# Sums of squares at five joints: six tiles added on GpSimd, three products of ones in place of eight

## The reference

```python
def rmsnorm_2(x, g):
    xf = x.astype(jnp.float32)
    y = xf * lax.rsqrt(jnp.mean(xf * xf, -1, keepdims=True) + EPS)
    return (y * g.astype(jnp.float32)).astype(x.dtype)

def macaron_half_ffn(x, pre_g, post_g, w_gate, w_up, w_down):
    h = rmsnorm_2(x, pre_g)
    h = (jax.nn.silu(h @ w_gate) * (h @ w_up)) @ w_down
    return x + 0.5 * rmsnorm_2(h, post_g)
...
    for i in range(DEPTH_2):
        p = layers[i]
        x = macaron_half_ffn(x, *p["ffn1"])
        pre_g, post_g = p["norms"]
        x = x + rmsnorm_2(p["mixer"](rmsnorm_2(x, pre_g), *p["mix"]), post_g)
        x = macaron_half_ffn(x, *p["ffn2"])
```

## Time and profile before

| | us |
|---|---|
| median of 3 runs | 2516.71 |
| lowest and highest run | 2516.51, 2528.49 |
| profiled execution, first to last instruction (span) | 2449.2 |
| median less span | 67.5 |
| TensorE busy in the span | 2190.0 (89%) |
| VectorE busy | 1628.7 (66%) |
| ScalarE busy | 997.5 (41%) |
| GpSimd busy | 541.4 (22%) |

### The profile page before, as it was taken

The page is one execution under the profiler, slowest core; times in us unless marked ns, Lnnn a source line. Parts: engine busy times, 40 slices in busy tenths (PEclk is TensorE's granted clock), DMA queues, the critical chain, the costliest instruction groups (busy, mean ns, idle before and its releaser), DMA issues. The chain is left out here.

```text
span 2449.2 us, 40856 instructions
## 1 busy us (share of the span) xinstructions
PE 2190.0 (89%) x16086; PEld 1805.2 (74%) x16086; DVE 1628.7 (66%) x3155; ACT 997.5 (41%) x1896; POOL 541.4 (22%) x549
## 2 busy tenths in 40 slices
PE   8988998877877777777999999999999898999998
PEld 7987998733332333224999988999999777888998
DVE  6675755766666676644766766666766777648666
ACT  5553535523333333333444445434444563024343
POOL 0000001877777777772100000000000000000000
PEclk9999999998899999999999999999999999999999
DMA  5530453899999999994655432655455432003653
GB/s 202 181 118 2 146 186 107 268 410 409 409 409 409 409 409 404 410 409 165 188 183 185 154 104 69 191 183 185 142 185 184 129 105 77 3 3 102 190 183 111
DMA packets 140319, 509.45 MB, mean 208 GB/s; under 512 B 15969, under 2 KB 16609, under 8 KB 139745
## 3 DMA queue, kind: packets, MB, share of 16 engines
q1 hardware_dynamic: 65824, 237.32, 30.4%
q0 software_dynamic: 73728, 268.47, 27.6%
q10 hardware_dynamic: 576, 1.05, 0.2%
HBM read 505.72 MB, written 1.05 MB: 207 GB/s over the span
## 5 line engine op out<-in xcount | busy, mean ns | idle before, releaser
L197 ACT ACTIVATE weights_high<-weights 128x1024 fp32r<-128x1024 f32 x436 | 460.2, 1059 | 532.5 <-PE ps L233 401.0
L231 PE MATMUL ps<-moving_high,weights_high 128*128 128x256 f32 x2224 | 639.8, 288 | 6.1 <-DVE moving_low L1277 3.0
L2284 PE MATMUL ps<-v_rows,subkeys 128*128 128x512 f32 x1024 | 494.7, 636 | 167.9 <-ACT subkeys L2338 167.9
L233 PE MATMUL ps<-moving_high,weights_low 128*128 128x256 f32 x2224 | 630.3, 283 | 0.0
L232 PE MATMUL ps<-moving_low,weights_high 128*128 128x256 f32 x2224 | 630.2, 283 | 0.0
L205 DVE TENSOR_TENSOR weights_low<-weights,weights_high 128x1024 fp32r<-128x1024 f32 x419 | 513.2, 1227 | 171.2 <-ACT weights_high L197 168.5
L2284 PEld LDWEIGHTS ps<-v_rows,subkeys 128*128 128x128 f32 x1024 | 200.6, 203 | 460.8 <-issue 460.7
L2444 DVE CUSTOM_DVE_ANT_0 u_rows<-u_rows,ps 128x1024 f32<-128x1024 f32 x256 | 308.9, 1219 | 233.2 <-DMA u_rows<-in_peer_u,experts 232.8
L231 PEld LDWEIGHTS ps<-moving_high,weights_high 128*128 128x128 f32 x2224 | 427.4, 192 | 11.4 <-issue 8.5
L232 PEld LDWEIGHTS ps<-moving_low,weights_high 128*128 128x128 f32 x2224 | 427.5, 192 | 0.6
L233 PEld LDWEIGHTS ps<-moving_high,weights_low 128*128 128x128 f32 x2224 | 427.1, 192 | 0.0
(11 more groups left out here) (569 smaller groups left out, 3198.2 us busy)
## 6 DMA issues: line engine op xcount, KB each, us to landing
weights<-in_l_ffn SPq DMA_DIRECT2D x264, 512.0 KB, 4.0
weights<-in_w_in SPq DMA_DIRECT2D x44, 512.0 KB, 4.0
weights<-in_l_in SPq DMA_DIRECT2D x24, 512.0 KB, 3.7
weights<-in_l_rkv SPq DMA_DIRECT2D x24, 512.0 KB, 3.6
weights<-in_w_ckv SPq DMA_DIRECT2D x16, 512.0 KB, 4.4
weights<-in_w_pq SPq DMA_DIRECT2D x16, 512.0 KB, 4.1
weights<-in_w_up_pair SPq DMA_DIRECT2D x8, 512.0 KB, 3.5
weights<-in_w_mix_out SPq DMA_DIRECT2D x8, 512.0 KB, 4.4
```

The source lines that it names most:

```text
L197: act.activation(self.high[:, c % SPLIT, :], self.raw[:, c % RING, :], ACT.Copy)\
L231: pe.matmul(out, lhs.high, rhs.high, start=start, stop=False)
L233: return pe.matmul(out, lhs.low, rhs.high, start=False, stop=stop)
L2284: last = pe.matmul(k.ps[:, 2 * tb + half, :], diagonal[:, i % DIAGONALS, :], v_rows[:, i % V_RING, 512 * half:512 * half + 512], start=i < ...
```

## The change

In each joint GpSimd now adds the squares of the first six tiles into tile 0, by five additions of 128x256: 1 to 0, then 3 to 2 and 2 to 0, then 5 to 4 and 4 to 0, each pair as soon as ScalarE has made its squares. TensorE makes no sums ahead of t = 2 and t = 4; ahead of t = 6 it waits for the last squares, makes the products of ones for tiles 6 and 7, waits for `six_added`, and makes the one for the sum of the six. `nsa_mixer`'s stage gets a GpSimd part that it did not have (`has_pool`).

```diff
--- before.py
+++ after.py
@@ -522,7 +522,7 @@
 
 
     order = (0, 1, 2, 4, 5, 6, 7, 3)
-    roots_first = False
+    roots_first, has_pool = False, True
     chunks = NSA_CHUNKS
     gain = "l0_mix_pre_g_2"
     GATES, CONV, CONV_GATE, KEYS, VALUES, QUERIES = (4, 5), 4, 12, 16, 18, 20
@@ -550,6 +550,9 @@
         h, tb = self.items[i]
         g = h // NSA_REP
         return h, tb, g, h % NSA_REP, P * (tb + 1), slice(64 * g, 64 * g + 64), slice(P * tb, P * tb + P)
+
+    def pool(self, pool, S):
+        late_parts_pool(pool, Front(S), self.squares)
 
     def ready(self, n):
         return n + 1
@@ -952,7 +955,7 @@
 
 
     order = range(KT)
-    roots_first = True
+    roots_first, has_pool = True, False
     chunks = 0
 
     def __init__(self, k, ctx, m, parts):
@@ -1084,6 +1087,11 @@
                 act.wait_ge(S["sum_ready"], 1)
                 act.activation(root[:, :], k.ps[:, sum_bank, 0:T], ACT.Sqrt, bias=k.eps(), scale=1.0 / D)\
                    .then_inc(S["root_ready"], 1)
+
+            if make.has_pool:
+                @block.gpsimd
+                def _(pool):
+                    make.pool(pool, S)
 
             @block.tensor
             def _(pe):
@@ -2452,17 +2460,14 @@
     keep_warm(k, pe, 6, 3)
     first_three = [k.w.arrived(pe) for _ in range(3)]
 
-    def sums(q):
-        pe.wait_ge(S["squares_ready"], q + 1)
-        for t in (2 * q, 2 * q + 1):
-            last = pe.matmul(k.ps[:, sum_bank, 0:T], k.const("ones"), squares[:, t, :], start=t == 0, stop=t == KT - 1)
-        return last
-
     for t in range(KT):
-        if t in (2, 4, 6):
-            sums(t // 2 - 1)
         if t == 6:
-            sums(3).then_inc(S["sum_ready"], 1)
+            pe.wait_ge(S["squares_ready"], 4)
+            for i in (6, 7):
+                pe.matmul(k.ps[:, sum_bank, 0:T], k.const("ones"), squares[:, i, :], start=i == 6, stop=False)
+            pe.wait_ge(S["six_added"], 1)
+            pe.matmul(k.ps[:, sum_bank, 0:T], k.const("ones"), squares[:, 0, :], start=False, stop=True)\
+              .then_inc(S["sum_ready"], 1)
         pe.wait_ge(S["parts_ready"], t + 1)
         for bank, tiles in enumerate(first_three):
             last = product(pe, k.ps[:, bank, 0:T], tiles[:, t, :], parts[:, t, :], start=t == 0, stop=t == KT - 1)
@@ -2476,6 +2481,20 @@
         for t in (2 * q, 2 * q + 1):
             act.activation(parts.high[:, t, :], src[:, t, :], ACT.Copy, scale=k.column(gain, t)).then_inc(S["high_ready"], 1)
         act.activation(squares[:, 2 * q:2 * q + 2, :], src[:, 2 * q:2 * q + 2, :], ACT.Square).then_inc(S["squares_ready"], 1)
+
+
+def late_parts_pool(pool, S, squares):
+    own = Steps(pool, S["pool_steps"])
+    for q in range(3):
+        pool.wait_ge(S["squares_ready"], q + 1)
+        own.did(pool.tensor_tensor(squares[:, 2 * q, :], squares[:, 2 * q, :], squares[:, 2 * q + 1, :], ALU.add))
+        own.settle()
+        if q:
+            added = pool.tensor_tensor(squares[:, 0, :], squares[:, 0, :], squares[:, 2 * q, :], ALU.add)
+            if q == 1:
+                own.did(added)
+            else:
+                added.then_inc(S["six_added"], 1)
 
 
 def late_parts_vector(k, v, S, src, gain, parts, update):
@@ -2668,6 +2687,7 @@
 
             @block.gpsimd
             def _(pool):
+                late_parts_pool(pool, S, squares)
                 if final:
                     pool.wait_ge(S["own_scale"], 1)
                     for q in range(4):
```

## The result

| | before | changed |
|---|---|---|
| median of 17 runs each, us | 2523.31 | 2530.98 |
| lowest to highest, us | 2515.06 to 2530.53 | 2516.24 to 2538.95 |
| profiled execution: time, us | not given | 2530.26 |
| profiled execution: span, us | 2449.2 | 2528.5 |

The ratio is 1.0037, with a 95% interval of 1.0026 to 1.0047: the change costs 9.3 us (6.6 to 11.9); the two medians differ by 7.7. Forecast were -0.15 us, 2516.6, and a range from 2510 to 2523. The loss was missed.

The account below looks back on a forecast made before the run. TensorE was taken as the late engine in the joints, VectorE having some three us to spare. Three FFN joints at 0.0, nsa_mixer +2.0 and l0_ffn1 -2.15 gave -0.15 us, on the median 2516.6 us, range 2510 to 2523.

Parts of the forecast that it names:

- What is removed: TensorE, all five joints: ten records of ones fewer per joint, 2.15 us each joint, 10.75 us in all, the ceiling.
- what is added: GpSimd, all five joints: five additions of 128x256 per joint, 25 in all, which stop VectorE.
- the stop of 0.54 us: VectorE in the joints: each GpSimd addition of 256 elements stops it 0.54 us, with ends 0.49 and 1.08.
- rival 3: Joints: the whole addition locks VectorE, 0.76 us each; FFN joints lose 0.2, nsa_mixer 3.1; +1.6, 2518.3 us; chance 0.12.
- The walk through an FFN joint: Joints before l0_ffn2, l1_ffn1, l1_ffn2: VectorE 2.0 us later, TensorE reaches tile 6 at 1362.24 against 1362.23; gain 0.0 each.
- rival 2: Joints: additions stop VectorE longer, 1.08 us each; FFN joints 1.5 us later, nsa_mixer loses 4.7; +7.0, 2523.7 us; chance 0.08.
- l0_ffn1: Joint where TensorE is far behind and VectorE has slack: the chain behind it moves ahead as a whole, -2.15 us.
- nsa_mixer's +2.0: Behind tile 6 of nsa_mixer's joint TensorE waits for VectorE, so all of VectorE's 2.0 us delay arrive: +2.0 us.
- rival 4: nsa_mixer and three FFN joints: new idle time lowers TensorE's clock, 1.56 us per fall; +6.2, 2522.8 us; chance 0.07.
- TensorE's freed time could not have been used here: nsa_mixer's joint: TensorE waits for VectorE behind tile 6, so freed time brings nothing even without GpSimd.
- Those 67.5 us lie outside of the span: Whole program: median 2516.71 us lies 67.5 above the profiled span of 2449.2, outside it and untouched by the change.
- No case reaches 12.6 us: Whole program: no rival nor the 10.75 us ceiling reaches 0.5%, 12.6 us; faster 0.02, slower 0.03, same 0.95.

Follow-up runs that it names:

- the run without additions: Changed kernel with all GpSimd additions dropped, so squares of tiles 1 to 5 are left out of the norm; ratio 1.0006 is not its own: 0.9979.
- the filled stop: Changed kernel with five unused identity products on TensorE where it stands still in nsa_mixer, ahead of the fifth weight chunk; ratio 1.0006 (0.9992 to 1.0020).

## Why the prediction was wrong

- **What is removed, what is added, and the stop of 0.54 us**: right. 0.55 each was measured, four of them, the fifth in ScalarE's shadow. Three rows from the begin of the trace, far from the joints, and the order of work written out, were enough. The rule quoted from the Trainium skill, page SBUF — State Buffer, section "SBUF: two separate sides", agrees with the trace in that one of the two blocks the other. But the fastest record of an addition is 0.740 us, and what it takes from VectorE is 0.55, so not the whole instruction, as far as GpSimd's records go, which are rough. That was rival 3, and it did not happen.
- **The walk through an FFN joint**: right, within 0.1 us in all three, and the run without additions shows that it is these stops that eat the 2.1 us.
- **The sums of rivals 2 and 3**: wrong. In the walk VectorE 2.0 us late leaves an FFN joint where it was, so each us beyond is lost. Rival 3 has VectorE 3.1 us late, which is 1.1 us a joint and not 0.2, and some +4.2 in all; rival 2 has 4.7, which is 2.7 a joint and not 1.5, and some +10.6. Neither happened, but both were priced too low.
- **l0_ffn1**: right, 2.16 us sooner for 2.15. The stage's own length moved by 2.8, of which nothing can be made, since it varies by 1.7 with nothing changed.
- **nsa_mixer's +2.0**: right as a wait (0.41 to 2.51 us) but it was put down as the stage's whole loss, and **this is the step that failed**: "All of VectorE's 2.0 us arrive at TensorE: +2.0 us", with nothing for the clock in the sum. The stage lost 11.4. The other 9.4 are the clock, as the filled stop shows. It was named as rival 4, with two errors. Its price was taken from one row of another stage (1.56 us), where dense wide products follow the stop; in nsa_mixer, gate products follow, and the price is six times that. And its chance was set at 0.07, since each new stretch was shorter than the 3.68 us of that row; but a row that shows a fall at 3.68 says nothing on 2.4, and the trace of the kernel before had nearer ones. The stop of 2.70 us at 1921.33 (above) was followed by a fall, and so was one of 2.33 us, whose next 20 us have a mean clock of 0.74, that is 10.2 us at the lower level:

```profile
2201.91 0.48 PE L988 MATMUL ps<-norms,spread 16*128 16x256 f32 x1 [2.33 <-DVE norms L1018]
```

- **"TensorE's freed time could not have been used here"**: right, and not harmless. In the run without additions the freed time alone brought the fall. By that run the change would have lost here in either way.
- **"Those 67.5 us lie outside of the span"**: wrong. In the changed kernel's profiled execution 1.8 us lie outside (2530.26 less 2528.5). The span of before was short by its expert layer. It did not enter the difference, but the median of 3 runs that the number was put on stands 6.6 us below that of 17, which moved the whole range down. The measured 2530.98 lies 14.4 us above 2516.6, and 6.6 of them are this base. On the right one the range would have ended at 2529.6, and the measured time would still lie above it.
- **"No case reaches 12.6 us"**: it held, at 9.3, though not by the reasons given.

## What to carry to other kernels

When a change makes an engine later in front of TensorE, or TensorE earlier in front of a wait, look up how long TensorE will stand still and what runs behind it: a wait grown by 2 us was worth 11 in the profiled executions here, and filling it with five products that nobody needs gave 9 of them back. Price a fall of the clock from the work that follows in that very place, not from another stage. And an addition handed to GpSimd beside a busy VectorE isn't free: 128x256 cost VectorE 0.55 us each, more than the 0.43 that the product of ones had cost TensorE, so it pays only where VectorE has slack. Two in an FFN joint gained 0.9 us by the stages, five gained 0.1, three weren't tried; nsa_mixer's joint has no slack. And a stage read from one profiled execution needs the time of many runs beside it: where the clock can fall, two executions of the same code differ.

## What was not expected of the hardware

- After a stop of 2.5 us the clock was at the lower level for 20.5 us while TensorE was busy all the time with wide products and two of 128x24 ahead of each tile; with wide products alone, after the same stop, for 3.4 us. In five kernels with stops from 0.36 to 1.11 us and that same mixture it did not fall.
- A stop of 1.83 us brought 17.1 us of the lower level, one of 2.52 us 17.1 in one kernel and 20.5 in another.
- The same stop of 2.70 us in the RWKV mixer was followed by a fall in nine profiled executions and by none in three.
- The expert layer took 722 us of one profiled execution and 791 of another with the same work, at 386 and 352 GB/s. That is more than any effect of the change, and the reason why the spans of two profiles can't be compared.
